# PEER layer of a two-layer diffusion trunk: the last sparse tile's top-k choice moved from the gate-table stage into the dense-row loop, with four tile buffers in place of five

## The reference, cut to what matters

```python
q = (xc @ wq).reshape(C, PEER_HEADS, 2, PEER_DKEY // 2)          # 8 heads, two halves
s = jnp.einsum('chzd,zkd->chzk', q, subkeys)                     # 128 keys per half
top_s, top_i = lax.top_k(s, 16)
cand_s = top_s[:, :, 0, :, None] + top_s[:, :, 1, None, :]       # 16 x 16 pair sums
best_s, best_j = lax.top_k(cand_s, 16)
idx = take(top_i[0] * 128 + top_i[1], best_j);  g = softmax(best_s)
act = gelu(einsum('cd,chkd->chk', xc, u[idx]))
y = einsum('chk,chkd->cd', g * act, v[idx])                      # 8 x 16 experts of 16384 per token
```

## Time and profile before

| what | value |
|---|---|
| median of three runs | 4784.03 us |
| the profiled execution's own time | 4783.03 us |
| its span (first to last instruction) | 4781.4 us |
| TensorE busy | 87% of the span |
| VectorE busy | 70% |
| ScalarE busy | 27% |
| GpSimd (gathers) busy | 37% |
| mean DMA rate | 294 GB/s |

### The profile page before, as it was taken

One profiled execution on the slowest core, in us unless ns is written; L12 is line 12 of the kernel. 1 busy time (PEld: TensorE's weight loads), 2 busy tenths in 40 slices (PEclk: granted clock), 3 DMA queues, 4 the chain that ended last, 5 costly groups with the idle time before them and its releaser, 6 DMA issues.

```text
span 4781.4 us, 53394 instructions
## 1 busy us (share of the span) xinstructions
PE 4179.8 (87%) x18407; PEld 2873.7 (60%) x18407; DVE 3339.1 (70%) x6731; ACT 1307.1 (27%) x2628; POOL 1767.5 (37%) x1652
## 2 busy tenths in 40 slices
PE   7999976694999899999999979886657779999997
PEld 3676664483676666666666645553443446666665
DVE  2466665568889677777777846775588767777776
ACT  3231311111666211111111123331214652222222
POOL 0012111022665455566565600000126655454452
PEclk8999978797999999999999989998778989999998
DMA  6966774713999999999999926888518999999995
GB/s 235 286 198 200 228 224 140 262 58 106 360 408 346 389 363 400 396 389 390 368 390 391 392 99 189 227 222 233 181 52 320 381 365 398 391 389 400 394 393 224
DMA packets 514579, 1408.04 MB, mean 294 GB/s; under 512 B 45693, under 2 KB 128893, under 8 KB 509471
## 3 DMA queue, kind: packets, MB, share of 16 engines
q1 hardware_dynamic: 330014, 733.73, 46.0%
q0 software_dynamic: 184320, 671.17, 36.2%
HBM read 1226.46 MB, written 178.26 MB: 294 GB/s over the span
## 4 chain that ended last, share of the span: by engine, by line
PE 65%; DVE 14%; DMA 10%; ACT 3%; POOL 3%; issue 3%; SPq 0%; DVEq 0%; ACTq 0%; POOLq 0%
PE ps L1840 20%; PE ps L1831 17%; DMA peer_arena<-in_peer_u 4%; PE ps L1804 3%; PE ps L1518 3%; DMA u_rows<-mixer_arena 3%; PE ps L746 3%; PE ps L1227 2%; PE ps L1232 2%; DMA expert_rows<-u_rows,peer_arena 2%; PE ps L321 2%; PE ps L749 2%; DVE expert_rows L2085 2%; PE ps L815 1%; DMA u_rows<-hidden 1%
## 5 line engine op out<-in xcount | busy, mean ns | idle before, releaser
L1787 POOL DMA_INDIRECT expert_rows<-u_rows,peer_arena x640 | 829.1, 1296 | 1052.5 <-DVE expert_rows L2085 821.8
L1831 PE MATMUL ps<-part_arena,peer_part_arena 128*128 128x384 f32 (+1 forms) x4096 | 1031.4, 334 | 37.7 <-DVE peer_part_arena L2128 25.4
L2085 DVE SCALAR_TENSOR_TENSOR expert_rows<-expert_rows,mixer_in 128x1024 f32<-128x1024 f32 x640 | 762.2, 1220 | 114.3 <-DMA expert_rows<-u_rows,peer_arena 112.0
L1794 POOL DMA_INDIRECT expert_rows<-in_peer_v,peer_arena x640 | 742.5, 1160 | 223.9 <-issue 186.5
L1831 PEld LDWEIGHTS ps<-part_arena,peer_part_arena 128*128 128x128 f32 x4096 | 699.7, 190 | 110.1 <-issue 99.0
L1840 PE MATMUL ps<-best,peer_arena 128*128 128x512 f32 x1540 | 685.3, 592 | 0.0
L1831 PE MATMUL ps<-mixer_in_parts,peer_part_arena 128*128 128x384 f32 (+1 forms) x2048 | 633.7, 309 | 0.0
L2110 DVE SCALAR_TENSOR_TENSOR peer_arena<-expert_rows,peer_arena 128x1024 f32<-128x1024 f32 x445 | 571.7, 1285 | 35.0 <-DVE peer_arena L2110 1.9
L1804 PE MATMUL ps<-expert_rows,peer_arena 128*128 128x512 f32 x768 | 387.8, 653 | 202.9 <-ACT peer_arena L1919 202.7
L1840 PEld LDWEIGHTS ps<-best,peer_arena 128*128 128x128 f32 x1540 | 285.1, 189 | 296.0 <-issue 296.0
L1571 POOL TENSOR_TENSOR part_arena<-peer_arena,part_arena 128x1024 fp32r<-128x1024 f32 x32 | 76.5, 2392 | 1007.1 <-ACT part_arena L1548 1007.1
(11 more groups left out here) (273 smaller groups left out, 6104.7 us busy)
## 6 DMA issues: line engine op xcount, KB each, us to landing
peer_arena<-in_peer_u SPq DMA_DIRECT2D x256, 512.0 KB, 12.1
best<-in_peer_v SPq DMA_DIRECT2D x154, 512.0 KB, 8.2
mixer_arena<-in_peer_u SPq DMA_DIRECT2D x272, 256.0 KB, 7.4
u_rows<-mixer_arena SPq DMA_DIRECT2D x136, 512.0 KB, 5.0
hidden<-in_peer_u SPq DMA_DIRECT2D x240, 256.0 KB, 6.2
u_rows<-hidden SPq DMA_DIRECT2D x120, 512.0 KB, 5.1
gates<-peer_arena SPq DMA_DIRECT2D x20, 2048.0 KB, 10.7
peer_arena<-in_peer_v SPq DMA_DIRECT2D x52, 512.0 KB, 7.6
```

The costliest lines, as they stand in the source:

```text
L1787: pool.indirect_dma_start(u_ring[:, k % U_SLOTS, :], None, u_table, bass.IndirectOffsetOnAxis(u_index[s][:, m:m + 1], 0)).then_inc(u_row_i ...
L1794: pool.indirect_dma_start(v_ring[:, k % V_SLOTS, :], None, v_table, bass.IndirectOffsetOnAxis(v_index[s][:, m:m + 1], 0)).then_inc(v_row_i ...
L1831: mm = pe.matmul(ps[:, 6, 0:dense_tok], left[j % len(left)][:, c, :], right[:, c, :], start=at == 0, stop=at == len(todo) - 1)
L2085: dve.scalar_tensor_tensor(out=rows, in0=rows, scalar=1.0, in1=B.x[:, :, rows_at + s * P:rows_at + s * P + P], op0=ALU.mult, op1=ALU.mult, ...
```

## The change

In the first layer (`LATE = 1`) the last choice, n = 5 (sparse tile 2), leaves the gate-table stage: `BESIDE` becomes (1, 1, 1). Its pieces run on DVE in the dense loop, one at the head of each row from row 4 on (before the row's groups): 6 of the search, then `decode` in four parts of two heads each (5 pieces a part), then the normalization, rows 4 to 30 in all. Its exponential on ACT comes at row 20. POOL's gathers of sparse tile 2 wait for all four parts. The waits on `chosen_ok` ask for five tiles in place of six. The moved choice has candidate and XOR space of its own in the PEER arena (`late_cand`, `late_differ`); for this u and v tiles have four buffers in the first layer (`BUFS = 4`). The second layer keeps five buffers and its order.

```diff
-    BUFS = 5
+    LATE = (1, 0)[layer]
+    BUFS = 5 - LATE
...
+    late_differ = [B.peer_arena[:, ar.at + 512 * z:ar.at + 512 * z + 512].bitcast(U32).rearrange("p (h k a) -> p h k a", h=2, a=TOPK)
+                   for z in range(2)]
     diag = [ar.take(P) for _ in range(V_SLOTS)]
...
+    if LATE:
+        kept_top = B.best[:, tiles * 2 * HEADS * TOPK:]
+        v_space = [v_space[0], B.best[:, 0:D], kept_top[:, 0:D], v_space[4]]
...
+    late_cand = [ar.take(HEADS * CAND).rearrange("p (h k) -> p h k", h=HEADS) for _ in range(2)] if LATE else None
...
-    BESIDE = [1] * (nd - 1) + [ns - 1]
+    BESIDE = [1] * (nd - 1) + [ns - 1 - LATE]
+    LATE_PARTS, LATE_FROM, LATE_EXP = 4, 4, 20
...
-        sp.wait_ge(chosen_ok, tiles)
+        sp.wait_ge(chosen_ok, tiles - LATE)
...
-                pool.wait_ge(index_ok, s + 2 if s else 1)
+                pool.wait_ge(index_ok, (s + 2 if s < ns - LATE else s + 1 + LATE_PARTS) if s else 1)
...
-        act.wait_ge(chosen_ok, tiles)
+        act.wait_ge(chosen_ok, tiles - LATE)
...
         for j in range(KEYS):
+            if LATE and j == LATE_EXP:
+                exp(tiles - 1)
             for a in groups_of(j):
                 gelus(a)
...
-            parts = 2 if n == 0 else 1
+            parts = 2 if n == 0 else LATE_PARTS if late(n) else 1
...
+        if LATE:
+            dve.wait_ge(g_mm, BATCH)
+        last = choose(tiles - 1) if LATE else iter(())
         for j in range(KEYS):
+            if LATE and j == LATE_FROM:
+                dve.wait_ge(s0_mm, first_rows)
+            if j >= LATE_FROM:
+                next(last, None)
             for a in groups_of(j):
                 products(a)
```

More of the change, by code:

```diff
@@ L1665, in peer @@
     cand_space = [spare.take(PAIRS * TOPK) for _ in range(2)]
-    cand = [x[:, 0:HEADS * CAND].rearrange("p (h k) -> p h k", h=HEADS) for x in cand_space]
-    differ = [x.bitcast(U32).rearrange("p (h k a) -> p h k a", h=HEADS, a=TOPK) for x in cand_space]
+    near_cand = [x[:, 0:HEADS * CAND].rearrange("p (h k) -> p h k", h=HEADS) for x in cand_space]
+    near_differ = [x.bitcast(U32).rearrange("p (h k a) -> p h k a", h=HEADS, a=TOPK) for x in cand_space]
     digit_u, bits = [ar.take(PAIRS, U32) for _ in range(2)], [ar.take(PAIRS, U32) for _ in range(4)]
@@ L1695, in peer @@
     u_high = [parts.take(C * P).rearrange("p (c i) -> p c i", c=C) for _ in range(2)]
+    ar.at = parts.at
+    late_cand = [ar.take(HEADS * CAND).rearrange("p (h k) -> p h k", h=HEADS) for _ in range(2)] if LATE else None
+    assert ar.at <= PEER_ARENA - 4 * PAIRS
     parts.at = at
@@ L1719, in peer, with late @@
     ORDER = [nd] + list(range(nd)) + list(range(nd + 1, tiles))
-    BESIDE = [1] * (nd - 1) + [ns - 1]
+    BESIDE = [1] * (nd - 1) + [ns - 1 - LATE]
     EXP_AT = [(16,) if x == 1 else (8, 20) for x in BESIDE]
     TURN_AT, TURNED_AT = LOTS - 5, LOTS - 3
+    LATE_PARTS, LATE_FROM, LATE_EXP = 4, 4, 20
+    def late(n):
+        return n >= tiles - LATE
     def which(tile):
@@ L1981, in search @@
         def search(n):
+            cand = late_cand if late(n) else near_cand
             here, best, best_j = top[:, ORDER[n]], kept[n % 2], kept_j[n % 2]
@@ L2014, in decode @@
             here_key = top_key[:, ORDER[n]]
+            differ = late_differ if late(n) else [x[:, HEADS * part // parts:HEADS * (part + 1) // parts] for x in near_differ]
             some, some_h = (slice(x * part // parts, x * (part + 1) // parts) for x in (PAIRS, HEADS))
@@ L2035, in decode @@
                 chain.inc(dve.tensor_tensor(
-                    differ[z][:, some_h], here_key[:, some_h, z, :].unsqueeze(2).to_broadcast([P, HEADS // parts, TOPK, TOPK]),
+                    differ[z], here_key[:, some_h, z, :].unsqueeze(2).to_broadcast([P, HEADS // parts, TOPK, TOPK]),
                     x.rearrange("p (h k) -> p h k", k=TOPK).unsqueeze(3).to_broadcast([P, HEADS // parts, TOPK, TOPK]),
@@ L2041, in decode @@
             for z in range(2):
-                chain.inc(dve.tensor_reduce(chosen[z][:, some], differ[z][:, some_h].rearrange("p h k a -> p (h k) a"), AX.X, ALU.min))
+                chain.inc(dve.tensor_reduce(chosen[z][:, some], differ[z].rearrange("p h k a -> p (h k) a"), AX.X, ALU.min))
                 yield
```

## The result

The changed kernel takes 4805.51 us, the median of 20 runs (4786.02 to 4819.54). The kernel before takes 4778.91 us, the median of 20 runs beside them (4768.26 to 4789.1). The ratio is 1.0056, with a 95% interval of 1.0046 to 1.0066: the change costs 26.6 us. That is slower by over 0.2%, and 2.5 us above the end of the predicted range (4803).

What follows compares the result with a forecast made beforehand. VectorE was taken to bound the gate-table stage's last batch, TensorE the dense loop. From the profiled 4783.03 us, -23.5 + 1 + 4.3 + 16 = -2.2 gave 4780.8, forecast as 4781, range 4763 to 4803.

Steps and rivals of the forecast that it cites:

- Part 4, four buffers: First layer's dense loop: u tiles issued one row later arrive late behind the gate slices; +16 us, between 6 and 27.
- the slack: Dense loop: lag a row takes without loss, 3.8 us with two groups, 8.9 us with one.
- a mean landing of 18.3 us: Dense loop: u tiles behind the gate slices land in 18.3 us, a VectorE lag of 5.3 us once in four rows.
- The upper end: Four-buffer loss in the dense loop: two two-group and three one-group rows meet landings of 25 to 26 us; 27 us.
- A TensorE that waits gives the next tile the same time back.: Dense loop: reason for taking the middle, 16 us, as the four-buffer loss although long landings occur.
- the rival: Dense loop: late u tiles pace it at split_u; stage gains 22.5, loop loses 46 us, time 4806.5; chance 0.18.
- Part 1, the last batch: Gate-table stage: with one choice less, the last batch runs at 3.55 us a lot; gain 23.5 us, between 18 and 24.2.
- Part 2, between stage and loop: Last gate write and first u tile lie on the path amid denser transfers; +1 us, within 0 and 2.
- Part 3, the choice in the loop: Dense loop: VectorE's moved pieces are covered on average, but TensorE waits around rows 19 and 20; +4.3 us, 0 to 12.
- landings above 22 us in most sets: Dense loop: u-tile landings that would show the slow case, late u tiles pacing the loop.

Runs made afterwards that it cites:

- u_ahead: Changed kernel with u tile j + 1 issued ahead of gate slices j and v tile j in the first layer, four buffers: 4759.22 us, ratio 0.9947.
- five_plain: Changed kernel with five u and four v buffers in the first layer, queue order unchanged (slices, u tile, v tile): 4797.4 us, ratio 1.0047.
- five_u: Changed kernel with five u and four v buffers in the first layer, u(j + 2) issued right behind v(j): 4760.98 us, ratio 0.9962.
- slices_after_u: Changed kernel with the gate slices issued behind u tile j instead of ahead of it in the first layer: 4768.33 us, ratio 0.9975.
- ahead_both: u_ahead with the same queue order in the second layer too, which keeps five buffers: 4743.35 us, ratio 0.9938.
- four_ahead: Kernel before, no moved choice, with four u and v buffers and u tile j + 1 issued ahead of slices j in the first layer: 4772.74 us, ratio 0.999.
- four_only: Kernel before with four u and v buffers in the first layer and nothing else, no moved choice: 4824.45 us, ratio 1.0085.

## Why the prediction was wrong

**Part 4, four buffers (+16; measured about +40): the step that failed, by its size.** The mechanism was as written. `split_u` stands before the row's products, they before ScalarE's gelus, and TensorE waits for those. The price past the slack held as well: in the set shown a landing of 22.6 us let TensorE lose 1.0 us, and the next one, of 25.5 us, let it wait 3.6 us, where the prediction has one us for each us above 22. u_ahead puts the price of the four buffers in the old order at 1243.0 - 1202.1 = 40.9 us. Three things in the term were wrong:

- How late the tiles are. I took a mean landing of 18.3 us, which is a lag of 5.3 us. The 26 late tiles of the changed kernel's loop land after 21.3 us in the mean (14.0 to 25.5, from SP's issue to ScalarE's rounding; the five others came in time), and by the prediction's own working that is a lag of 8.3 us: a row of two groups (slack 3.8) then loses 4.5 us and not 1.5, and the 13 tiles that land after more than 22 us pass the slack of the other rows. The upper end counted five. In the kernel before the 30 landings are 18.5 us in the mean, near the 18.3 that I read, but they run from 12.8 to 26.2, with five above 22.
- The clock, which stood at nothing. Of the 44.1 us of the loop, 31.8 are more waiting of TensorE for the gelu of the scores (37.1 against 5.3), and 12.2 are scores that ran slower after such a wait.
- "A TensorE that waits gives the next tile the same time back." The next u tile leaves when TensorE's own values end, so it leaves later by just the time TensorE lost, and the sets follow one another 39.5 us apart on average.

My upper end of 27 us lay below the 40.9. It was in the rival's price (46) only, and I gave that 0.18.

I also treated buffers and order as one question. The section on the kernel before says that u(j + 1) stands behind v(j) in the queue; the prediction then works out the issue "when values(j - 5) end" from the count alone and never asks what another order would give. five_plain shows it: five u buffers and 1247.5 us.

**Part 1, the last batch (-23.5; measured about -13): overstated.** The lots were counted wrongly. I took TensorE's row at 1426.79 to follow lot 61. `turn` gives TensorE its three transposes beside lot 59 (they are VectorE's that come two lots later), so the stretch to lot 95 holds 36 lots. At the pace of 3.55 us a lot that is 127.9 us, a gain of 17.1 us and not 24.2. TensorE's timeline in the changed kernel has the same two points:

```profile
1419.90 0.49 PE L1825 MATMUL ps<-identity,peer_arena 128*128 128x128 f32 x3
1420.59 3.70 PE L1818 MATMUL ps<-expert_rows,peer_arena 128*128 128x512 f32 x8 [0.20 <-ACT peer_arena L1933]
...
1554.77 7.13 PE L1818 MATMUL ps<-expert_rows,peer_arena 128*128 128x512 f32 x16 [0.59 <-ACT peer_arena L1933]
```

That is 134.2 us in place of 145.0; in five_u, slices_after_u and u_ahead it is 130.1, 131.5 and 133.5, so 132.3 in the mean and a gain of 12.7 us. What keeps it some 4 us above the pace of the batch before isn't shown; in this execution one modulation tile took 14.11 us to land and stood on the chain, and the granted clock was 0.97. The first scores came 18.5 us sooner in the pair of profiles (6.2 of it already there before lot 59, which is the scatter between two executions), and 16.6 us sooner in the mean of six profiles with the moved choice against three without. Part of the 16.6 is the order of the queue: from lot 95 to the first scores slices_after_u, u_ahead and ahead_both take 13.6 to 13.9 us, the three kernels with the moved choice that issue the slices first 16.4 to 17.4.

The Trainium skill's rule that HBM binds at about 358 GB/s ("DMA: Bandwidth & Descriptors", section "Where 436 GB/s comes from") would have given a time of 4802, nearer the result than mine. It is no support for the rule: the trace doesn't agree, since the last batch ran at 391 GB/s and did get shorter. The time came out there for another reason.

**Part 2, between stage and loop (+1; measured -1.5).** Gate write and first u tile took 6.30 and 6.04 us against 7.76 and 6.12; from lot 95 to the first scores 16.5 us in place of 18.0. The step was wrong in sign and small.

**Part 3, the choice in the loop (+4.3; measured +5.0).** Right, by u_ahead against four_ahead, and in the place given: TensorE at 194.8 of 200 us around rows 12 to 33 in the changed kernel and in u_ahead. It is the price where the u tiles are in time; in the old order, beside late tiles, the times show none (four_only).

**The sum.** With the measured terms it is -12.7 - 1.5 + 5.0 + 40.9 = 31.7 us; the medians say 26.6, and unchanged code alone differed by more than this gap between two executions (18.7). The time came out at the rival's 4806.5, for a partly wrong reason: the rival's gain in the stage was too large by some 8 us, and its loss in the loop (46 us) close to right. As its sign I had named "landings above 22 us in most sets". The runs show 13 of 31 sets: not most, but with the slower scores after the waits it was enough.

**What stays open.** By their ratios u_ahead is faster than four_ahead by 0.0043, 20.5 us, with some 9 us of uncertainty on either side. The first layer explains some 11.6 of it in the means over the profiles (16.6 less 5.0), and only 3.4 in the pair of profiles itself: their loops end at 2786.86 and 2790.24 us, while the spans differ by 18.1. The rest lies in code that isn't touched, above all in the second layer's gate-table stage. From the first matmul of its query projection (L1518) to its loop's first values it takes 510.3, 508.4 and 502.9 us in the three profiles without the moved choice (before, four_only, four_ahead), and 491.7 to 501.4 us in the six with it. Whether this is scatter or an effect of the order of the earlier work wasn't tried. Whether the landings behind the slices as a whole got longer isn't settled either: the 21.3 us are the mean of the late ones alone, and the 18.5 of the kernel before that of all.

## What to carry to other kernels

Before a buffer is given up, compute for each transfer the time from its issue to its need, and read from the queue what it stands behind: the wait of the entry ahead of it may set its issue, and then one buffer more buys nothing while one change of the order buys it all. Put the tile that is needed soonest ahead of a large transfer that has rows of time. And where the issue of a late tile waits for the engine that the tile delays, price the loss as one that repeats in every period, not as one that is given back, and read what TensorE's clock does after each gap.

## What the runs showed of the hardware

An issue of SP that directly follows the gate slices holds SP's queue for several microseconds: 8.32 us in the set shown, 6.3 us in the mean of the 29 sets of the changed kernel's loop (1.5 to 8.5), and 6.3 in the kernel before as well, while other issues of u and v tiles take 0.5 us in the mean. In u_ahead the u tile's issue ahead of the slices takes 0.33 us, and the next one after the slices is a v tile that waits for TensorE and comes 4.8 us later; it takes 1.8 us in the mean of its 30 sets:

```profile
1734.63 0.33 SPq L1788 DMA_DIRECT2D peer_arena<-in_peer_u  x1
1735.00 0.43 SPq L1781 DMA_DIRECT2D peer_arena<-gates  x1
1739.78 2.01 SPq L1794 DMA_DIRECT2D peer_arena<-in_peer_v  x1
```

So whatever is issued next gets through some 7 us after the slices' issue (0.5 + 6.3, 4.8 + 1.8), and a tile right behind them starts with that handicap. In slices_after_u, where it comes 9 us later, it takes 1.2 us. The Trainium skill, "DMA: Bandwidth & Descriptors", section "Queues, rings and completion order", says that each DMA engine takes up the descriptors of a ring in their order. The trace agrees as far as it shows: the tile behind the slices lands after 22.5 us on average where it is on the chain (a choice of the late ones), and once it stands ahead of them the waits for it fall from 28 to 3.

A wait of TensorE can cost more than its own length: 5 of the 18 scores behind a wait in the changed kernel's loop took 5.9 to 7.1 us. Those at 2545 us, after a wait of 3.6 us, took 7.13 us at a granted clock of 0.59, against 4.22 us at full clock.

The changed kernel also scatters more from run to run than the one before (33.5 us between the extremes of 20 runs, against 20.8).
